# Query norms of neighbourhood and differential attention: the rate moved from the query tiles into the softmax's row scale

## The reference, cut to what matters

```
def rms_norm_2(x, g):
    xf = x.astype(jnp.float32)
    y = xf * lax.rsqrt(jnp.mean(xf * xf, axis=-1, keepdims=True) + EPS)
    return (y * g.astype(jnp.float32)).astype(x.dtype)
...
na_q = rms_norm_2(na_q.reshape(lead + (NA_HEADS, HEAD_DIM)), na_q_g)
na_k = rms_norm_2(na_k.reshape(lead + (NA_HEADS, HEAD_DIM)), na_k_g)
dq = rms_norm_2(dq.reshape(lead + (DIFF_HEADS, 2, DIFF_D)), diff_q_g)
dk = rms_norm_2(dk.reshape(lead + (DIFF_HEADS, 2, DIFF_D)), diff_k_g)
...
s_lat = jnp.einsum('bnqhd,bnkhd->bhnqk', qr, kb).astype(jnp.float32) * NA_SCALE + bias
...
p = jax.nn.softmax(jnp.concatenate([s_ctx, s_lat], axis=-1), axis=-1)
...
s = jnp.einsum('bqhmd,bkhmd->bhmqk', q, k).astype(jnp.float32) * scale
p = jax.nn.softmax(s, axis=-1)
a = (p[:, :, 0] - lam * p[:, :, 1]).astype(v.dtype)
```

## Time and profile before

| | |
|---|---|
| median of 3 runs | 2367.08 us (2366.32 to 2367.88) |
| profiled execution, own time | 2367.78 us |
| its span, first to last instruction | 2365.7 us |
| PE, DVE, ACT, POOL busy | 97%, 66%, 51%, 18% of the span |
| granted TensorE clock, mean | 0.996 of full speed |

### The profile page before, as it was taken

One profiled execution on the slowest core, in us unless ns is written; L12 is line 12 of the kernel. 1 busy time (PEld: TensorE's weight loads), 2 busy tenths in 40 slices (PEclk: granted clock), 3 DMA queues, 4 the chain that ended last, 5 costly groups with the idle time before them and its releaser, 6 DMA issues. The chain is left out here.

```text
span 2365.7 us, 35055 instructions
## 1 busy us (share of the span) xinstructions
PE 2300.6 (97%) x13726; PEld 1906.2 (81%) x13726; DVE 1570.2 (66%) x2382; ACT 1214.6 (51%) x2096; POOL 425.3 (18%) x275
## 2 busy tenths in 40 slices
PE   8998999999999999999999999999999999999999
PEld 5776788887888888799998767777777888778888
DVE  5967989768766666687676554643576465574675
ACT  2666554313328434667454345764376253576384
POOL 0000000000006446000002431004201126404301
PEclk9999999999999999999999999999999999999999
DMA  9734527666544333446664231213222334334344
GB/s 317 238 113 154 159 81 213 179 194 190 157 135 126 98 89 89 142 124 186 191 183 125 74 92 56 68 49 86 72 72 81 89 95 122 89 99 122 86 115 139
DMA packets 419339, 301.01 MB, mean 127 GB/s; under 512 B 13442, under 2 KB 389352, under 8 KB 419176
## 3 DMA queue, kind: packets, MB, share of 16 engines
q1 hardware_dynamic: 418064, 298.33, 43.8%
q10 hardware_dynamic: 1112, 0.44, 0.1%
HBM read 297.68 MB, written 1.05 MB: 126 GB/s over the span
## 5 line engine op out<-in xcount | busy, mean ns | idle before, releaser
L243 ACT ACTIVATE weights_hi<-wslots 128x1024 fp32r<-128x1024 f32 (+1 forms) x408 | 425.0, 1047 | 214.0 <-PE psum L306 180.1
L306 PE MATMUL psum<-input_hi,weights_hi 128*128 128x512 f32 (+1 forms) x1376 | 486.1, 353 | 4.0 <-ACT gla_gate L1921 2.3
L306 PE MATMUL psum<-input_hi,weights_lo 128*128 128x512 f32 (+1 forms) x1376 | 474.5, 345 | 0.0
L306 PE MATMUL psum<-input_lo,weights_hi 128*128 128x512 f32 (+1 forms) x1376 | 474.0, 344 | 0.0
L253 DVE TENSOR_TENSOR weights_lo<-wslots,weights_hi 128x1024 fp32r<-128x1024 f32 x277 | 339.7, 1235 | 116.3 <-ACT weights_hi L243 115.2
L253 POOL TENSOR_TENSOR weights_lo<-wslots,weights_hi 128x1024 fp32r<-128x1024 f32 (+1 forms) x128 | 305.9, 2398 | 570.6 <-ACT weights_hi L243 570.4
L306 PEld LDWEIGHTS psum<-input_hi,weights_hi 128*128 128x128 f32 x1376 | 258.5, 188 | 45.8 <-issue 9.5
L306 PEld LDWEIGHTS psum<-input_lo,weights_hi 128*128 128x128 f32 x1376 | 258.7, 188 | 33.9 <-issue 2.6
L306 PEld LDWEIGHTS psum<-input_hi,weights_lo 128*128 128x128 f32 x1376 | 258.4, 188 | 32.9
L306 PE MATMUL psum<-ffn_hidden_hi,weights_hi 128*128 128x512 f32 (+1 forms) x512 | 172.3, 336 | 0.0
L306 PE MATMUL psum<-ffn_hidden_hi,weights_lo 128*128 128x512 f32 (+1 forms) x512 | 170.8, 334 | 0.0
(11 more groups left out here) (615 smaller groups left out, 4876.7 us busy)
## 6 DMA issues: line engine op xcount, KB each, us to landing
wslots<-w_in SPq DMA_DIRECT2D x130, 512.0 KB, 3.9
wslots<-ffn_w SPq DMA_DIRECT2D x128, 512.0 KB, 4.5
wslots<-ssd_w_in SPq DMA_DIRECT2D x49, 512.0 KB, 4.0
wslots<-ada_w SPq DMA_DIRECT2D x32, 512.0 KB, 4.7
h<-w_ada SPq DMA_DIRECT2D x28, 512.0 KB, 4.3
wslots<-gla_w_in SPq DMA_DIRECT2D x24, 512.0 KB, 4.7
input_raw<-ada_w SPq DMA_DIRECT2D x24, 512.0 KB, 4.0
ada_slab<-ada_w SPq DMA_DIRECT2D x24, 512.0 KB, 3.9
```

Of the source, the lines that this page charges most:

```text
L243: act.activation(self.high(self.whi_r, n), self.slot(n), ACT.Copy)\
L306: ins = pe.matmul(out_of(self.bank(g)), l, r, start=first and i == 0, stop=last and i == len(pairs) - 1, skip_group_check=not (first and l ...
```

## The change

For the query tiles of the two kinds, PE no longer spreads the sums over a head's partitions. It uses the squares as the stationary operand, one 128-token piece at a time, and two columns of the ones matrix as the moving one, so that the sums come out by token: 128 tokens on the partitions, two numbers beside each other. All 16 pieces (8 in layer 1) gather in one PSUM bank. ACT takes one small square root of them, after the last product, and DVE one small reciprocal and a multiplication by 1/8; they stay in 32 columns of an old tile (`mod1`). The query tiles get the gain alone. In the attention stages the row scale of the exponentials, the factor before the bias and the factor of the negated maximum are no longer constants of the instruction but are read from these columns, one number per partition. The keys' norms stay; their waits are counted anew.

```
+QUERY_SUMS = 6
+def query_rates(b):
+    return b.mod1[:, 0, 0:4 * TT, :].rearrange("p (n t) a -> p n t a", n=4)
+
+def sum_by_query(b, pe, n, sq, cols):
+    pe.wait_ge(b.sem("squared"), b.nth("squared", n + 1))
+    sums = b.psum[:, QUERY_SUMS, 0:4 * TT * 2].rearrange("p (n t a) -> p n t a", n=4, t=TT)
+    for t in range(cols[0] // P, cols[1] // P):
+        c = t * P - cols[0]
+        ins = pe.matmul(sums[:, n, t, :], sq[:, n % 2, c:c + P], b.half_ones[:, 0:P:P // 2], start=n == 0 and c == 0,
+                        stop=n == 3 and t == cols[1] // P - 1, skip_group_check=True)
+    ins.then_inc(b.tick("square_added"), 1)
+
+def query_deviation(b, act, cols):
+    act.wait_ge(b.sem("square_added"), b.nth("square_added", 4))
...
+    act.activation(query_rates(b)[:, :, t, :], sums[:, :, t, :], ACT.Sqrt, bias=b.eps[:, 1:2], scale=1.0 / 64)\
+        .then_inc(b.tick("query_deviation"), 1)
+
+def query_rate(b, dve, cols):
+    x = query_rates(b)[:, :, cols[0] // P:cols[1] // P, :]
+    dve.wait_ge(b.sem("query_deviation"), b.nth("query_deviation", 1))
+    dve.reciprocal(x, x).then_inc(b.tick("dve_step"), 1)
+    dve.wait_ge(b.sem("dve_step"), b.all("dve_step"))
+    dve.tensor_scalar(x, x, 64 ** -0.5, None, ALU.mult).then_inc(b.tick("query_rates"), 1)
+
+def gain_queries(b, dve, n, x, gain):
+    dve.wait_ge(b.sem("squared"), b.nth("squared", n + 1))
+    dve.tensor_scalar(x, x, gain, None, ALU.mult).then_inc(b.tick("normed"), 1)
...
@@ project_heads, PE
-                    if n >= lag:
+                    if lag <= n < lag + 4:
+                        sum_by_query(b, pe, n - lag, sq, cols[n - lag])
+                    elif n >= lag:
                         sum_for_norm(b, pe, n - lag, b.half_ones[:], sq, cols[n - lag])
@@ project_heads, ACT
-                    if n >= 3:
-                        deviation_for_norm(b, act, n - 3, rstd, P, cols[n - 3], 64)
+                query_deviation(b, act, seg)
+                deviation_for_norm(b, act, 4, rstd, P, cols[4], 64)
                 b.round_weights(act, v0 + VS - 1)
@@ project_heads, DVE
-                for n in range(8):
-                    scale_for_norm(b, dve, n, tile(n), rstd, P, cols[n], column(b, gains[n // 4], l))
+                for n in range(4):
+                    gain_queries(b, dve, n, tile(n), column(b, gains[0], l))
+                query_rate(b, dve, seg)
+                for n in range(4, 8):
+                    scale_for_norm(b, dve, n, tile(n), rstd, P, cols[n], column(b, gains[1], l))
@@ attend_pairs, with rate(n, a) = a column of query_rates
+                        sc = 1.0 if n < NEAR else rate(n, a) if near else scale
...
-                            dve.scalar_tensor_tensor(biased[:, a, :], src, scale, bias[:, a, :], ALU.mult, ALU.add)\
+                            dve.scalar_tensor_tensor(biased[:, a, :], src, rate(n, a), bias[:, a, :], ALU.mult, ALU.add)\
...
+                            dve.tensor_scalar(top[:, n % 2, a, 1:2], top[:, n % 2, a, 0:1], rate(n, a), -1.0, ALU.mult, ALU.mult)\
@@ attend_maps
-                                       bias=top[:, n % 2, a, 1:2], scale=scale, accum_out=den[:, n % 2, a:a + 1])\
+                                       bias=top[:, n % 2, a, 1:2], scale=rate(n, a), accum_out=den[:, n % 2, a:a + 1])\
...
-                        dve.tensor_scalar(top[:, n % 2, a, 1:2], top[:, n % 2, a, 0:1], -scale, None, ALU.mult)\
+                        dve.tensor_scalar(top[:, n % 2, a, 1:2], top[:, n % 2, a, 0:1], rate(n, a), -1.0, ALU.mult, ALU.mult)\
```

More of the change, by code:

```diff
@@ L3243, in sum_for_norm @@
     pe.wait_ge(b.sem("squared"), b.nth("squared", n + 1))
-    if n >= 2:
-        pe.wait_ge(b.sem("deviation_ready"), b.nth("deviation_ready", n - 1))
+    if n >= 6:
+        pe.wait_ge(b.sem("deviation_ready"), b.nth("deviation_ready", n - 5))
     w = cols[1] - cols[0]
@@ L3248, in sum_for_norm @@
         .then_inc(b.tick("square_added"), 1)
+QUERY_SUMS = 6
[11 more added lines that the diff above has]
+    act.wait_ge(b.sem("square_added"), b.nth("square_added", 4))
+    sums = b.psum[:, QUERY_SUMS, 0:4 * TT * 2].rearrange("p (n t a) -> p n t a", n=4, t=TT)
+    t = slice(cols[0] // P, cols[1] // P)
+    act.activation(query_rates(b)[:, :, t, :], sums[:, :, t, :], ACT.Sqrt, bias=b.eps[:, 1:2], scale=1.0 / 64)\
[9 more added lines that the diff above has]
+    dve.tensor_scalar(x, x, gain, None, ALU.mult).then_inc(b.tick("normed"), 1)
 def square_for_norm(b, pool, n, g, x, sq, rows, cols):
@@ L3270, in scale_for_norm @@
     r = rstd[0:rows, n % 2, 0:w]
-    dve.wait_ge(b.sem("deviation_ready"), b.nth("deviation_ready", n + 1))
+    dve.wait_ge(b.sem("deviation_ready"), b.nth("deviation_ready", n - 3))
     dve.reciprocal(r, r).then_inc(b.tick("dve_step"), 1)
@@ L3798, in qcols, with rate @@
             return slice(seg[0] + t * P, seg[0] + (t + 1) * P)
+        def rate(n, a):
+            gq, p = units[n]
+            t = qcols(gq).start // P
+            return query_rates(b)[:, p, t, a:a + 1]
         def start(n):
@@ L3914, in exps @@
                         k = keys(n)
-                        src, sc = (biased[:, a, :], 1.0) if n < NEAR else (b.psum[:, SCORE[a], 0:k], scale)
+                        src = biased[:, a, :] if n < NEAR else b.psum[:, SCORE[a], 0:k]
+                        sc = 1.0 if n < NEAR else rate(n, a) if near else scale
                         act.activation(prob[:, n % 2, a, 0:k], src, ACT.Exp, bias=top[:, n % 2, a, 1:2], scale=sc,
@@ L3928, in _ @@
                     act.wait_ge(b.sem("normed"), b.nth("normed", 0))
+                    act.wait_ge(b.sem("query_rates"), b.nth("query_rates", 0))
                 fill.scalar_first(act)
@@ L3943, in _ @@
                     dve.wait_ge(b.sem("bias_cleared"), b.nth("bias_cleared", 0))
+                    dve.wait_ge(b.sem("query_rates"), b.nth("query_rates", 0))
                 def maxima(n):
@@ L3962, in maxima @@
                         dve.wait_ge(b.sem("top_made"), b.nth("top_made", 2 * n + a + 1))
-                        dve.tensor_scalar(top[:, n % 2, a, 1:2], top[:, n % 2, a, 0:1], -1.0 if n < NEAR else -scale, None,
-                                          ALU.mult).then_inc(b.tick("top_ready"), 1)
+                        if n < NEAR or not near:
+                            dve.tensor_scalar(top[:, n % 2, a, 1:2], top[:, n % 2, a, 0:1], -1.0 if near else -scale, None,
+                                              ALU.mult).then_inc(b.tick("top_ready"), 1)
+                        else:
+                            dve.tensor_scalar(top[:, n % 2, a, 1:2], top[:, n % 2, a, 0:1], rate(n, a), -1.0, ALU.mult, ALU.mult)\
+                                .then_inc(b.tick("top_ready"), 1)
                 def normalise(n):
@@ L4278, in attend_maps @@
 def attend_maps(b, l, m, last, fill):
-    scale = 64 ** -0.5
     groups = [(s, t) for s in ((LAT,) if last else (LAT, CTX)) for t in range(2)]
@@ L4299, in qcols, with rate @@
         return slice(s[0] + t * P, s[0] + (t + 1) * P)
+    def rate(n, a):
+        gq, h = units[n]
+        return query_rates(b)[:, h, qcols(gq).start // P, a:a + 1]
     def start(n):
```

2 lines of the change are left out of this document (1 added, 1 removed).

## The result

Beside the kernel before on one chip the changed kernel took 2376.04 us in the median of six runs (2373.65 to 2377.46), the kernel before 2367.48 (2366.06 to 2372.73). The ratio is 1.0028, with a 95% interval of 1.0018 to 1.0039: +6.6 us, +4.3 to +9.2. So the change makes the kernel slower, by about the bound that the prediction named or a little more. The forecast of 2369.5 was too low, and the first median lies 3 us above the range.

What follows compares the result with a forecast made beforehand. PE was taken to bound the projection stages, with waits on DVE or ACT in attention. DVE and ACT 0, PE's sums +0.4 and operands +2.0 gave +2.4 us, 2369.5 us on the median of 2367.08; range 2365.5 to 2373.0.

Steps and rivals of the forecast that it cites:

- the bound that the prediction named: Whole kernel: a measurement can tell about 0.2%, 4.7 us, from no change.
- forecast for operands: Attention stages: PE pays 0.4 and 0.2 us in neighbourhood attention, 0.5 and 0.9 in differential, layers 0 and 1.
- the operands' 2.0 us: Attention stages: scale read per partition costs 0.12 or 0.23 us in each unit where PE already waits, 2.0 us together.
- the 9.3 us offered: Attention stages: operand cost if none is hidden, 32 x 0.23 + 16 x 0.12 us.
- Nothing hidden, slower: Attention loops: every operand paid in full, +9.7 us, 2376.8; over 46% paid puts it beyond the bound; chance 0.10.
- 0.45 to about 0.7: Differential attention of layer 1: PE's waits before the turns grow from 0.45 to about 0.7 us.
- DVE's relief, worth nothing: Query norms in projection stages: 40.8 us of DVE reciprocals disappear, priced at nothing because PE's products hide them.
- DVE's relief reaches PE: Wait of 5.22 us at 2014.90: less DVE backlog removes most, 2364.3 us; chance of faster, by relief or something unseen, 0.05.
- PE's sums, +0.4 us: Projection stages: narrow sums cost +0.03 us per tile in layer 0, half in layer 1; other bound -1.3 us.
- The move is covered: Projection stages: later root and key norms cost nothing; the rival that they do, 2371 to 2372.5 us, had 0.05.
- the four further units: Differential attention of layer 1: the other four units begin to wait too, at most another 0.9 us.
- an uncovered root: Projection stages: the later root delays the rounded value weights until PE waits, one loss of 1.6 us.

Runs made afterwards that it cites:

- kernel after, 1st: Profiled execution of the changed kernel, from its first measurement against the kernel before: 2376.04 us, ratio 1.0028; the profiled execution itself took 2374.76 us.
- kernel after, 2nd: The changed kernel, unaltered, measured and traced again with more runs beside the kernel before: 2373.89 us, ratio 1.0020.
- operands alone: Kernel before with its norms, but exponentials, biased scores and negated maximum read the constant 0.125 from the rate columns: 2374.03 us, ratio 1.0024.
- exponential alone: Kernel before with only ScalarE's exponentials reading the constant scale from columns, VectorE's two operations keeping their constants: 2370.43 us, ratio 1.0013.
- VectorE's alone: Kernel before with only VectorE's biased scores and negated maximum reading the constant scale from columns: 2369.47 us, ratio 1.0004.
- projection side alone: Changed kernel with the constant scale in the attention stages, query norms still made but not applied: 2367.48 us, ratio 0.9998 against the kernel before.
- before, new order: Kernel before with VectorE negating the first maximum right behind its own reduction: 2364.59 us, ratio 0.9984.
- after, new order: Changed kernel with VectorE negating the first maximum right behind its own reduction: 2370.28 us, ratio 1.0007 against the kernel before.
- the kernel with the shorter loop: Changed kernel with the first maximum negated at once and near projection l0's sums one tile later: 2369.50 us, ratio 1.0001 against the kernel before.
- the run meant for it: Kernel before with the exponential's column operand, plus one small ScalarE operation ahead of each differential exponential: 2386.97 us, ratio 1.0077 against the kernel before.

## Why the prediction was wrong

Here is by how much each trace is later than that of the kernel before at the end of a stage, less its lag at the stage's start, in us, from the starts of PE's instructions. The cuts are the first turn of the near units of layer 0 and the first scores and last turn of each differential stage. So `near l0` holds latent attention and the next projection of layer 0 too, and `between` holds the near units of layer 1:

```
                         near l0   diff l0   between   diff l1   sum
kernel after, 1st          1.5       1.6       0.2       1.8     5.1
kernel after, 2nd          1.4       1.7       0.0       1.7     4.8
operands alone             0.8       1.7       2.1*      2.1     6.7
exponential alone          0.1       1.4       0.3       1.8     3.6
VectorE's alone            0.5       0.4      -0.4       0.7     1.2
projection side alone      0.2       0.1      -0.3       0.1     0.1
before, new order         -0.7      -0.1      -1.8      -1.5    -4.1
after, new order          -0.1       0.9      -1.4      -0.1    -0.7
forecast for operands      0.4       0.5       0.2       0.9     2.0
```

\* The granted clock fell to 0.66 in 2080 to 2090 us of that execution, in a projection stage.

- **The term that failed is the operands' 2.0 us.** Each price was right within 0.01 us: 775 ns for the exponential, 747 for the biased scores, 208 instead of 148 for the negated maximum. The exposure was too small by more than half: 4.8 us in the second trace of the kernel after, 5.7 us measured for the operands alone, so 50 to 60% of the 9.3 us offered, not 21%. That is past the 46% from which the rival *Nothing hidden, slower* decides, though not its 9.3. The step that failed is the one from PE's waits to the price: the forecast charged each unit in which PE waited once, with one unit's 0.12 or 0.23 us. (One of the two waits that it charged in layer 1's neighbourhood attention is the 5.22 us for `mla_cq_lo`, which is no wait for this loop.) The traces show three things that it left out. The lag adds up from unit to unit where ACT and DVE pace them, and PE pays it at the last one, whose wait went from 0.69 to 1.52 us in layer 0 and from 0.41 to 1.14 in layer 1. A unit that had no wait began to wait (0.59 at 1768.52 us, more than the 0.23 of one unit). And part of it is paid before the next scores (`ACT prob`, from 0.5 us in the kernel before to 1.1 in layer 1), which the forecast never counted, since it listed the waits before the turns alone. Its sign "0.45 to about 0.7" was wrong for that reason: those stayed at 0.45.
- **The share that is paid differs from stage to stage.** The rival had the right stage for it: it named the chain that ended last, which runs through ACT and DVE alone in the differential attention of layer 1. That chain from the first rope operation to the last turn, in the kernel before and after:

```profile
2241.70 0.42 DVE rope_tmp L3289
...
2295.25 0.66 PE psum L4340 x4
```

```profile
2246.58 0.42 DVE rope_tmp L3328
...
2301.94 0.66 PE psum L4399 x4
```

It takes 53.55 us before and 55.36 after, 1.81 more, and 8 units of 0.23 us offered 1.84. There nothing is hidden, while the forecast charged 0.9. In the differential attention of layer 0 the chain of the kernel after runs through PE's products for a part of the units (1730.61 to 1749.36 and 1768.52 to 1785.80 us), and 1.6 to 1.7 of 3.7 us came out (forecast 0.5). In neighbourhood attention it was 1.4 to 1.5 of 2.8 us in layer 0 (0.8 with the operands alone; forecast 0.4) and 0.0 to 0.2 of 1.0 in layer 1 in the two traces of the kernel after.
- **DVE's relief, worth nothing: right in the time, wrong in size.** The projection side alone is at 0.9998, and even the kernel with the shorter loop did not profit. *DVE's relief reaches PE* is refuted: the wait for `mla_cq_lo` stayed at 5.0 us. But only 21 of the 40 us went. The prediction had the gain multiplication cheaper than the three-operand one that it replaces. The 16 of them take 34.7 us, and all such products of queries and keys together went from 42.2 us to 55.3. The small operations on the rates add 3.8 us, the longer operands most of the rest.
- **PE's sums, +0.4 us: not contradicted.** A tile's sum is 0.79 us long in the chain, and the chain has 0.79 + 5.61 us for sum and 24 products (0.86 + 5.49 before), so 0.05 us a tile. The projection side alone is within 0.5 us of before.
- **The move is covered**, as forecast: PE's waits in the projection stages are the same (1.1 us for GpSimd's first squares in both kernels).
- **The clock.** The fall at 1284 us in the first trace is not a steady part of the change. With the narrow sums behind the wait it came in two of four traces (the first of the kernel after, and the kernel after with the new order, 0.89 each), in neither the second of the same kernel nor the projection side alone. The six traces with wide sums there don't have it, which is too few to say that the narrow sums have no part in it. The mean granted clock over the timed runs of the second comparison is 0.9937 for either kernel. I take the excess of the first comparison (+6.6) over the second (+4.7) to be such chance; their intervals overlap.
- **The range.** Its upper end is not the sum that it was said to be: the forecast with the four further units and an uncovered root gives 2369.5 + 0.9 + 1.6 = 2372.0, not 2373.0. The measurement lies above either.

Open: in neighbourhood attention of layer 0 the two halves give 0.8 and 0.2 us and the whole 1.4. The same loop there runs through the bias buffers and GpSimd, and no run takes the rest apart. Open too is the true exposure for a small clean dose, since the run meant for it moved the table loads.

## What to carry to other kernels

An operand of 0.06 to 0.09 us is not free when it sits in a loop over engines: take the added time of one unit times the number of units that the loop paces (8 x 0.23 us in the last stage, of which 1.8 us came out), find out by the chain which stages the loop paces, and look at the last unit of a stage, where the lag is paid, not only at the units in which PE waits today. Relief is worth something only on the engine, and in the stage, where a wait ends. And before work is taken off the loop's engines, look at their order: negating the first maximum at once gave 3.8 us for one line taken out of each loop, nearly as much as the change lost.

## What the hardware showed that was not expected

- A TENSOR_SCALAR on 128x512 numbers took 2598 ns. One with two operands on as many numbers takes 0.55 us in the differential units, where GpSimd has no split. The slow one starts at 1284.95 and ends at 1287.52, and GpSimd's split beside it runs from 1284.87 to 1287.24; each of the four in layer 0's near projection stands beside such a split and ends just after it:

```profile
1284.95 2.57 DVE L3287 TENSOR_SCALAR att_qk<-att_qk,cols 128x512 f32<-128x512 f32 x1 [2.90 <-POOL head_sq L3295]
```

```profile
1284.87 2.37 POOL L253 TENSOR_TENSOR weights_lo<-wslots,weights_hi 128x1024 fp32r<-128x1024 f32 x1
```

The same instruction on 128x256 numbers shows both cases within the differential projection of layer 1. The first of the four starts at 2175.46, before its split (2175.75), and takes 0.35 us; the next starts after its split (2178.68) and takes 2.46:

```profile
2175.46 0.35 DVE L3287 TENSOR_SCALAR att_qk<-att_qk,cols 128x256 f32<-128x256 f32 x1 [1.62 <-POOL head_sq L3295]
2178.76 2.46 DVE L3287 TENSOR_SCALAR att_qk<-att_qk,cols 128x256 f32<-128x256 f32 x1 [2.96 <-POOL head_sq L3295]
```

It cost nothing here, as nobody waited for it. The Trainium skill (VectorE: DVE Perf Modes, section Two Vector instructions with no wait between them) names a second read interface of SBUF that VectorE's two-port modes share with GpSimd. The rows fit that, and the second trace of the kernel after has the same pair (0.35 and 2.47 us), but no run here took GpSimd's split away.

- An ACT table load runs ahead of the wait of the instruction that needs it (2291.46, with the exponential waiting until 2293.39), and is hidden as far as that wait lasts; put a small instruction with that wait in front, and the 1.28 us come after the wait. That holds where there is a wait: in the kernel with the exponential's operand alone, the exponential starts 0.27 to 1.59 us after the end of its load in 5 of 13 cases, and 0.02 us or less after it in the other 8. The Trainium skill (ScalarE: Activation LUTs, section What ACT_TABLE_LOAD costs) puts a switch of tables at 1.28 us and a drain of 1.38 together. Here the load starts at the end of the instruction before it (2302.61 + 0.20), and the exponential starts 1.30 us after the load's start (2302.81 to 2304.11), so no such drain shows.
- The same program's granted clock falls at different places from one execution to the next, each time for some microseconds: 0.66 in 1260 to 1270 us and 0.83 in 1280 to 1290 in the first trace of the kernel after, 1.00 in both in the second, which has 0.90 and 0.92 in 330 to 350 instead. Between two profiled executions of the kernel after this lie 3.4 us of span (2372.7 and 2369.3), more than half of what was to be explained. A single pair of traces is not enough for a change of this size; the waits, which are the same in both, are.
